# The row factor of the gated feed-forward's up half, applied at the residual instead of to each of its 22 tiles

## The reference

```python
def rmsnorm(x, g):
    xf = x.astype(jnp.float32)
    y = xf * lax.rsqrt(jnp.mean(xf * xf, axis=-1, keepdims=True) + EPS)
    return y.astype(x.dtype) * g
...
def swiglu(h, w_gu, w_down):
    gu = h @ w_gu
    g, u = gu[..., :D_FF], gu[..., D_FF:]
    return (jax.nn.silu(g) * u) @ w_down
...
        x = x + 0.5 * swiglu(rmsnorm(x, ffn1_norm[l]), ffn1_w_gu[l], ffn1_w_down[l])
```

## Time and profile before

| | |
|---|---|
| time, median of 3 executions | 3178.37 us (3172.16 to 3180.13) |
| the profiled execution: time | 3178.07 us |
| the profiled execution: span from its first to its last instruction | 3176.3 us |
| TensorE busy (matmuls) | 3037.3 us, 96% |
| VectorE busy | 1452.9 us, 46% |
| ScalarE busy | 964.2 us, 30% |
| GpSimd busy | 186.7 us, 6% |
| mean granted TensorE clock | 0.972 of full |

### The profile page before, as it was taken

How to read it: one execution, slowest core, us unless ns; L and a number is a source line. 1 busy time by engine, 2 the same in 40 slices (tenths; PEclk the granted TensorE clock), 3 DMA queues, 4 the chain that set the end, 5 groups by cost and what they waited for, 6 DMA issues and landing times.

```text
span 3176.3 us, 33719 instructions
## 1 busy us (share of the span) xinstructions
PE 3037.3 (96%) x13342; PEld 2260.0 (71%) x13342; DVE 1452.9 (46%) x2068; ACT 964.2 (30%) x1453; POOL 186.7 (6%) x179
## 2 busy tenths in 40 slices
PE   8999999999999999999999999889799999999997
PEld 6888774688887888775588887336588344588885
DVE  4434556543445443564544444343433754344444
ACT  3222424432234222333532223222223101232223
POOL 1000111100001000021010000000000520000000
PEclk9999999999999999999999999899599999999999
DMA  3222320122222222221032222211000121222222
GB/s 137 88 97 93 106 87 14 44 96 99 97 88 94 92 99 99 93 94 47 1 106 97 90 93 99 87 60 60 1 1 2 40 80 60 100 98 97 99 89 80
DMA packets 47276, 246.36 MB, mean 78 GB/s; under 512 B 5496, under 2 KB 5816, under 8 KB 24144
## 3 DMA queue, kind: packets, MB, share of 16 engines
q1 hardware_dynamic: 45632, 238.62, 21.5%
q10 hardware_dynamic: 1152, 6.24, 0.5%
q0 software_dynamic: 400, 0.23, 0.0%
HBM read 243.06 MB, written 2.10 MB: 77 GB/s over the span
## 4 chain that ended last, share of the span: by engine, by line
PE 85%; DVE 8%; ACT 3%; DMA 1%; issue 1%; POOL 1%; SPq 0%; DVEq 0%; ACTq 0%; POOLq 0%; PEldq 0%
PE psum L428 85%; DVE ring_lo L1582 1%; DVE stat L1760 1%; DMA ring<-in_wmix 1%; PE psum L745 1%; POOL scr L2204 1%; DVE scr L1768 0%; DVE scr L2032 0%; ACT highs L1185 0%; DVE scr L2088 0%; DVE hid L1749 0%; DMA x<-in_x 0%; ACT highs L1230 0%; DVE highs L1582 0%; DVE scr L1745 0%
## 5 line engine op out<-in xcount | busy, mean ns | idle before, releaser
L428 PE MATMUL psum<-highs 128*128 128x512 f32 (+1 forms) x3776 | 1331.0, 390 | 27.0 <-DVE ring_lo L1582 18.4
L428 PE MATMUL psum<-highs,ring_lo 128*128 128x512 f32 x2392 | 932.9, 390 | 0.0
L428 PEld LDWEIGHTS psum<-highs 128*128 128x128 f32 x3776 | 707.3, 188 | 185.7 <-issue 36.5
L428 PE MATMUL psum<-h_lo,highs 128*128 128x512 f32 x1952 | 762.1, 390 | 0.0
L1582 DVE TENSOR_TENSOR ring_lo<-ring,highs 128x2048 fp32r<-128x2048 f32 (+3 forms) x163 | 354.6, 2179 | 781.0 <-ACT highs L1230 704.1
L428 PEld LDWEIGHTS psum<-highs,ring_lo 128*128 128x128 f32 x2392 | 449.8, 188 | 95.6
L428 PEld LDWEIGHTS psum<-h_lo,highs 128*128 128x128 f32 x1952 | 367.2, 188 | 77.2 <-issue 0.5
L1230 ACT ACTIVATE highs<-ring 128x2048 fp32r<-128x2048 f32 x110 | 206.5, 1877 | 563.5 <-DMA ring<-in_wgu 540.1
L428 PE MATMUL psum<-h,ring 128*128 128x512 f32 x704 | 313.6, 602 | 9.2 <-DMA cst<-in_cst 8.2
L428 PEld LDWEIGHTS psum<-h,ring 128*128 128x128 f32 x704 | 135.6, 194 | 185.4 <-issue 175.9
L1582 DVE TENSOR_TENSOR highs<-hid,highs 128x512 fp32r<-128x512 f32 x220 | 155.3, 706 | 211.1 <-ACT highs L1257 118.5
(11 more groups left out here) (339 smaller groups left out, 2733.2 us busy)
## 6 DMA issues: line engine op xcount, KB each, us to landing
ring<-in_wgu SPq DMA_DIRECT2D x105, 1024.0 KB, 4.9
ring<-in_wmix SPq DMA_DIRECT2D x26, 1536.0 KB, 6.5
wdr<-in_wd SPq DMA_DIRECT2D x110, 256.0 KB, 2.7
ring<-in_wd SPq DMA_DIRECT2D x25, 1024.0 KB, 4.8
ring<-in_wmix SPq DMA_DIRECT2D x18, 1024.0 KB, 4.9
ring<-in_wgu SPq DMA_DIRECT2D x10, 512.0 KB, 5.0
mixw<-in_wsmall ACTq DMA_DIRECT2D x3, 1280.0 KB, 5.4
ring<-in_wd SPq DMA_DIRECT2D x5, 512.0 KB, 3.6
```

The source lines that it names most:

```text
L428: return nc.tensor.matmul(o, w, r, start=start, stop=stop, skip_group_check=True)
```

## The change

The up half is no longer multiplied by r tile by tile. `hid` is the silu'd gate times the raw up half, read straight from PSUM. The down projection then yields a sum without r, and `residual` applies it: one instruction multiplies the bank by the scale and by `rms_r` into `up_r`, and a second adds `up_r` to `x`. A wait between the two makes sure that `up_r` is written; a wait ahead of the first makes sure that the previous addition has read `up_r`. The residuals of the mixers stay as they are.

```diff
+AFTER_FFN = (1, 3, 4, 6, 9)
...
-            def residual(m, bank, ready, value, scale):
+            def residual(m, bank, ready, value, scale, row=None):
                 dve.wait_ge(ready, value)
+                if row is not None:
+                    dve.wait_ge(x_upd, row[1])
+                    nc.vector.scalar_tensor_tensor(out=up_r, in0=psum[:, bank, :], scalar=scale, in1=rms_r,
+                                                   op0=ALU.mult, op1=ALU.mult).then_inc(up_scaled, 1)
+                    dve.wait_ge(up_scaled, row[0])
+                    nc.vector.tensor_tensor(x[:, m, :], x[:, m, :], up_r, ALU.add).then_inc(x_upd, 1)
+                    return
                 nc.vector.scalar_tensor_tensor(out=x[:, m, :], in0=psum[:, bank, :], scalar=scale, in1=x[:, m, :],
                                                op0=ALU.mult, op1=ALU.add).then_inc(x_upd, 1)
...
                     dve.wait_ge(ring_free, used(n0 + j))
-                    nc.vector.tensor_tensor(up_r, psum[:, b + 2 + s, :], rms_r, ALU.mult).then_inc(up_scaled, 1)
-                    dve.wait_ge(up_scaled, f * NJ + j + 1)
                     dve.wait_ge(silu_ready, f * NJ + j + 1)
-                    nc.vector.tensor_tensor(hid[:, j, :], probs[:, s, :], up_r, ALU.mult).then_inc(hid_ready, 1)
+                    nc.vector.tensor_tensor(hid[:, j, :], probs[:, s, :], psum[:, b + 2 + s, :], ALU.mult).then_inc(hid_ready, 1)
...
-                        residual(*first_half[EARLY_RESIDUAL[k]])
+                        residual(*first_half[EARLY_RESIDUAL[k]], (KD * f + EARLY_RESIDUAL[k] + 1, KD * AFTER_FFN[f] + EARLY_RESIDUAL[k]))
...
-                        residual(4 + m, b + m, down_ready, 6 * f + m + 4, scale)
+                        residual(4 + m, b + m, down_ready, 6 * f + m + 4, scale, (KD * f + 5 + m, KD * AFTER_FFN[f] + 4 + m))
...
-                        residual(7, b + 3, ring_free, used(n0 + FFN_ITEMS - 1), scale)
+                        residual(7, b + 3, ring_free, used(n0 + FFN_ITEMS - 1), scale, (KD * f + KD, KD * AFTER_FFN[f] + 7))
```

## The result

The changed kernel takes 3189.07 us (median of 8 runs, 3184.68 to 3191.58), against 3178.2 us for the kernel before, measured beside it (8 runs). The ratio is 1.0033, 95% interval 1.0024 to 1.0042: slower by 10.9 us. A second set of 6 runs gave 1.0038 [1.0026, 1.0051]. The profiled execution took 3184.77 us, of which 3183.0 are the span; it is one of the fastest of its eight.

The account below looks back on a forecast made before the run. TensorE, busy 96% of the span, was taken as the bound, with VectorE counting only where TensorE waits for it. -2.45 + 8.4 + 1.8 + 5.7 = +13.45 us on 3178.07 us gave 3191.5 us, range 3184 to 3198.

Parts of the forecast that it names:

- The products in the loop are hidden: Inside the feed-forward loops, removing the 110 products by r was claimed to gain nothing, because TensorE's matmuls cover them.
- The end of the loop, -2.45 us: At tile 21 of all five stages, hid starts earlier and TensorE's wait of 0.49 us vanishes: -2.45 us.
- The seams, +8.4 us: At the end of stages 0 to 2, four added additions make residual 7 2.8 us late: +8.4 us, bounds 7.2 and 9.6.
- the 0.45 us of the weight loads: Ahead of the two mixers, row-sum weight loads wait 0.45 us for GpSimd; with 2.8 us added, waits of 3.25 us.
- The middle, +1.8 us: Residuals 0 to 3 of stages 0 to 2 delay the weight split, 0.6 us per stage: +1.8 us.
- both meetings with GpSimd: In the middle of stages 0 to 2, two VectorE instructions stretched by GpSimd's additions, claimed to fall on new additions.
- The clock, +5.7 us: Behind the three longer seam stops TensorE was expected at 1.2 GHz, 1.9 us each: +5.7 us, bounds 0 and 3.4 each.
- The rival in which the clock holds: TensorE's clock does not fall behind the seams: +7.75 us, 3185.8 us, slower by 0.24%; chance 0.17.
- The end of stages 3 and 4, nothing: The longer residuals there cost nothing beside TensorE's sums of squares; ScalarE's idle shrinks from 4.00 to 0.9 us.

Follow-up runs that it names:

- experiment 3: Changed kernel with the up half multiplied by r in the loop as before, so the factor is applied twice; 3188.99 us, 1.0044 of the kernel before.
- experiment 4: Changed kernel with the four late products in four scratch tiles, none waiting for an earlier addition; 3186.26 us, 1.0027 of the kernel before.
- experiment 2: Changed kernel with residuals 0 to 3 of every stage as the one old instruction, without the row factor; 3186.70 us, 1.0041 of the kernel before.
- experiment 7: Kernel before with r multiplied into the silu'd gate instead of the up half, residuals of one instruction; 3177.07 us, ratio 1.0005, and 0.9972 when run again.
- experiment 9: Kernel before with r on the silu'd gate and the four late one-instruction residuals ahead of all low parts; 3173.32 us, ratio 0.9980.
- experiment 5: Changed kernel with four scratch tiles and, at a stage's end, all low parts behind the last addition; 3181.56 us, 1.0012 of the kernel before.
- experiment 6: Kernel before with two unread products into scratch ahead of residual 7 of stages 0 to 2; 3182.46 us, ratio 1.0018.

## Why the prediction was right, and where its terms were off

The forecast was 3191.5 us with 3187.5 to 3195.5 as its own range, and 3189.07 came, by the mechanism that it named: VectorE's tail before the last `x` grows, and everything behind it to TensorE's row sums is late by as much. The nearness of the number is in part luck, for the middle was put too high and the clock a little too low.

- *The products in the loop are hidden.* Right: the loops run at 0.227 us per matmul in all kernels, and with the 110 products put back (experiment 3) only the end of the loop changes.
- *The end of the loop, -2.45 us.* Right in kind, a little small. The 0.49 us per stage are those of experiment 3. Matched matmul by matmul (both kernels have the same 13342), the changed kernel gains 0.54 to 0.61 us per stage, 2.9 us in all: the later steps of tile 21 wait a little less as well.
- *The seams, +8.4 us.* Right, though by its own words the upper bound should be higher: 0.1 us more for each of eight instructions is 0.8 us on top of 2.8, so 3 x 3.6 us and not 3 x 3.2. The last residual ended 2.83 us later against the first's start, and the waits grew by 3.42 - 0.61 = 2.81 us at the second seam. For the mixers I forecast 3.25 us and got 2.76: I took the 0.45 us of the weight loads for a wait of the matmuls, but in the kernel before the matmuls ran on until the row sums started. The delay of 2.8 us was right, only what it was added to was not. The term comes from the pairs, and here a page can be weighed. The Trainium skill, "VectorE: DVE Perf Modes", section "The DRAIN you can't avoid", says that a semaphore behind each of a chain of VectorE operations costs nothing extra. If each of the chain also waits for the one ahead, which the page does not say, the trace disagrees: a pair whose second instruction waits for the first is 0.72 us from start to start, two that don't wait 0.60 us, and without these waits each seam was 0.63 to 0.70 us shorter (experiment 4). With free waits the term would have been the 7.2 us of its lower bound.
- *The middle, +1.8 us.* The mis-sized term (its upper bound is 3 x 1.6 us by its own numbers, not 3 x 1.5). It measured 0.4 us: changed kernel less experiment 2, 0.11, 0.15 and 0.14 us at k = 10, and experiment 3 less the kernel before gives 0.1 us in the second and third stages as well (304.83 and 304.87 against 304.75 and 304.74). The first stage of the kernel before can't be used for this: in its profile TensorE waited 1.86 us ahead of k = 10, and the chain shows a transfer there,

```profile
339.98 6.98 DMA ring<-in_wd
```

  where the kernels of experiments 2, 7 and 9 waited 1.19 to 1.20 us as in the other stages. I had costed new work against the idle time rightly, but charged both meetings with GpSimd to the new additions. One meeting fell on a low part as before (1.78 us), and the other on an addition, where it stretched the instruction by 0.39 us only and freed the low part behind it, which had been stretched before. TensorE's wait at the split became shorter by 0.25 us because TensorE itself came later: in the second stage the low part of `hid` for k = 9 was done 300.23 us behind the loop's start, and 299.72 us in the kernel before, and the matmuls that need it start 0.3 us later against the steps ahead of them. Without that delay (experiment 2) the wait is 1.20 us again. GpSimd is stretched in these meetings too: its two additions there took 1.73 and 1.71 us, and 1.29 us each before.
- *The clock, +5.7 us.* Right in kind; 6.8 us by stretch, 6.4 us if the matmuls of both traces are matched. No seam cost the 1.9 us that I took for each: they cost 1.6, 3.2 and 1.6 us, and in the second profile 3.4, 3.4 and 1.7 us of full-speed time are missing, so the term itself scatters. Over all runs the mean clock of the changed kernel is 0.971 (14 runs), and that of the kernel before in the three sets 0.973 (64 runs); 0.002 of 3180 us is 6 us. The rival in which the clock holds is out. It fell behind waits half as long too (experiments 5 and 6), with one exception, 1.80 us in experiment 6. The trace of before had a warning that the prediction did not use: the wait of 1.86 us ahead of the matmul at 353.04 us did not cost the clock (1.00 over 345:365 us).
- *The end of stages 3 and 4, nothing.* Right: 0.75 us of idle are left where 0.9 were forecast, because a residual of two instructions takes 1.53 us to the next, not 1.46, for the wait on the addition ahead costs something after all.

The terms as measured: -2.9 + 8.4 + 0.4 + 6.4 = +12.3 us, against 10.9 between the medians (interval 7.6 to 13.3). The two profiled executions differ by 6.7 us only. The late transfer in the profile of before takes 0.7 us of the difference, and its first loop starts 0.5 us later; most of the rest is the clock in the mixers. In the second mixer the matmul that starts at 1479.66 us before starts at 1491.24 after, and the next 39 take 16.4 us there and 12.1 here. The granted clock of these stretches is 0.62 and 1.00 (columns as above):

```profile
1478.00:1496.00 18.00, 14.35 (x40) 7.74 (x40) 9.40 (x24) 8.05 (x21) 7.03 (x6) 0.62 0.00 0
```

```profile
1490.00:1508.00 18.00, 13.67 (x60) 7.10 (x60) 11.60 (x31) 9.88 (x30) 6.61 (x6) 1.00 0.00 0
```

It is scatter and not the change: in the second profile of the changed kernel, which took 3191.99 us, the same place has

```profile
1496.00:1514.00 18.00, 14.53 (x45) 7.05 (x45) 10.83 (x27) 8.83 (x25) 6.97 (x6) 0.72 0.00 0
```

## What to carry to other kernels

An instruction that is removed inside a covered loop is worth only what its last turn is worth, and four that are added in front of a chain which is already last cost their whole length, and here a fallen clock on top. Before a factor is moved out of a loop, see what the place that takes it stands in front of; here the same 0.5 us per stage were to be had by putting the factor on the operand that is ready first. Below 0.3%, compare waits in the trace and not times alone: one and the same kernel moved by 0.3% against its partner from one set of runs to the next, with the granted clock. And where two profiles are matched, look first for what only one execution met, such as the late transfer here.

## What was not expected of the hardware

- TensorE's clock fell to 1.2 GHz behind waits of 1.14 us ahead of both mixers, where every second group of three matmuls just before it had weights of 128x70, but stood at 1.00 behind a wait of 1.80 us in the same kernel, where all had been of 128x128 (experiment 6). Waits of 1.51, 1.52 and 2.12 us ahead of the row sums cost it as well (experiment 5). Waits of 1.20 us ahead of k = 10 did not, nor did one of 1.86 us at that place in the first stage of the kernel before. So a stream that looks busy to the last matmul can lose its clock behind little more than a microsecond. Whether the narrow weights are the reason was not tried.
- Behind the waits of experiment 5 (1.51, 2.12 and 1.52 us) 1.7 us of full-speed time are missing at each place, about as much as the waits themselves; behind the 3.42 us wait 3.4 us are missing. The clock fell only after TensorE had started again.
- Two VectorE instructions of 128x512, the second waiting for the first, are 0.72 us from start to start, and 0.60 us without the wait, each being 0.69 us long by the profile. Reading one operand from PSUM or both from SBUF made no difference (0.69 us each).
